# ScalarE rounds the next gate item's weights before it waits for the product

## The reference

```
h = rms_norm(x, ffn_pre_norm[l])
up = dwconv3(h @ w_up[l], ffn_conv_w[l], ffn_conv_b[l])
gate, val = jnp.split(up, 2, axis=-1)
f = (jax.nn.gelu(gate, approximate=True) * val) @ w_down[l]
x = x + rms_norm(f, ffn_post_norm[l])
```

## Time and profile before

| | |
|---|---|
| profiled execution, its time | 1559.35 us |
| its span, first to last instruction | 1557.6 us |
| PE busy | 1450.2 us, 93% |
| DVE busy | 882.8 us, 57% |
| ACT busy | 610.3 us, 39% |
| POOL busy | 520.5 us, 33% |
| mean granted clock of PE | 0.97 of full speed |
| up projection, first layer | about 398 to 652 us |
| up projection, second layer | about 1159 to 1413 us |
| DMA of an item of `w_up`, issue to landing | 3.8 us, median of 88 |

### The profile page before, as it was taken

The page is one execution under the profiler, slowest core; times in us unless marked ns, Lnnn a source line. Parts: engine busy times, 40 slices in busy tenths (PEclk is TensorE's granted clock), DMA queues, the critical chain, the costliest instruction groups (busy, mean ns, idle before and its releaser), DMA issues.

```text
span 1557.6 us, 14970 instructions
## 1 busy us (share of the span) xinstructions
PE 1450.2 (93%) x5815; PEld 1062.1 (68%) x5815; DVE 882.8 (57%) x1001; ACT 610.3 (39%) x859; POOL 520.5 (33%) x243
## 2 busy tenths in 40 slices
PE   5989989988999999999989898999989999999997
PEld 3667756556777777778746675554757777777885
DVE  4765677554676676611175666666456776774112
ACT  5222355643533433422242224556344344333222
POOL 2221311015444344344442122100354344344444
PEclk8999989999999999999989998999999999999998
DMA  7121200002133332323231112000213323322332
GB/s 245 41 57 38 61 28 1 1 28 81 54 87 89 95 90 86 92 88 98 88 126 50 41 45 71 1 0 1 68 41 95 94 83 95 94 82 89 97 95 71
DMA packets 195167, 108.53 MB, mean 70 GB/s; under 512 B 5895, under 2 KB 193657, under 8 KB 194202
## 3 DMA queue, kind: packets, MB, share of 16 engines
q1 hardware_dynamic: 195098, 107.58, 23.4%
HBM read 105.47 MB, written 2.10 MB: 69 GB/s over the span
## 4 chain that ended last, share of the span: by engine, by line
PE 51%; DVE 28%; ACT 14%; issue 5%; POOL 1%; DMA 0%; DVEq 0%; SPq 0%; ACTq 0%; POOLq 0%
PE ps L846 11%; PE ps L848 11%; PE ps L847 11%; DVE cv L1583 11%; ACT cv L753 4%; DVE cv L1586 4%; ACT wh L459 4%; PE ps L1104 3%; PE ps L937 2%; PE ps L824 2%; DVE nm L1485 2%; DVE fprod L1595 2%; PE ps L898 2%; PE ps L924 2%; DVE fl L1597 2%
## 5 line engine op out<-in xcount | busy, mean ns | idle before, releaser
L400 POOL TENSOR_TENSOR wl<-raw,wh 128x1024 fp32r<-128x1024 f32 x184 | 446.1, 2425 | 904.0 <-ACT wh L459 904.0
L846 PE MATMUL ps<-gh,wh 128*128 128x512 f32 x960 | 407.1, 424 | 10.2 <-POOL wl L400 9.2
L847 PE MATMUL ps<-gl,wh 128*128 128x512 f32 x960 | 380.3, 396 | 0.0
L848 PE MATMUL ps<-gh,wl 128*128 128x512 f32 x960 | 380.2, 396 | 0.0
L459 ACT ACTIVATE wh<-raw 128x1024 fp32r<-128x1024 f32 x184 | 193.5, 1052 | 399.5 <-PE ps L848 399.4
L1583 DVE SCALAR_TENSOR_TENSOR cv<-pad,pm,cv 128x512 f32<-128x512 f32 x88 | 179.5, 2040 | 119.2 <-ACT cv L753 119.2
L846 PEld LDWEIGHTS ps<-gh,wh 128*128 128x128 f32 x960 | 180.0, 187 | 83.4 <-issue 39.1
L847 PEld LDWEIGHTS ps<-gl,wh 128*128 128x128 f32 x960 | 180.1, 188 | 53.4 <-issue 12.8
L848 PEld LDWEIGHTS ps<-gh,wl 128*128 128x128 f32 x960 | 179.4, 187 | 45.5
L1215 DVE TENSOR_TENSOR acc<-acc,sq 128x512 f32<-128x512 f32 x24 | 60.5, 2522 | 192.5 <-ACT sq L493 192.3
L846 PE MATMUL ps<-fh,wh 128*128 128x512 f32 x352 | 139.3, 396 | 3.9 <-ACT wh L459 3.0
(11 more groups left out here) (216 smaller groups left out, 1855.1 us busy)
## 6 DMA issues: line engine op xcount, KB each, us to landing
raw<-w_up SPq DMA_DIRECT2D x88, 512.0 KB, 3.8
raw<-w_down SPq DMA_DIRECT2D x32, 512.0 KB, 3.6
raw<-w_in SPq DMA_DIRECT2D x30, 512.0 KB, 3.9
raw<-w_out SPq DMA_DIRECT2D x16, 512.0 KB, 3.7
raw<-w_down SPq DMA_DIRECT2D x16, 384.0 KB, 3.1
xio<-x SPq DMA_DIRECT2D x4, 512.0 KB, 4.3
win<-c_win SPq DMA_DIRECT2D x2, 1024.0 KB, 4.9
TF<-c_tf SPq DMA_DIRECT2D x2, 1024.0 KB, 9.5
```

The source lines that it names most:

```text
L400: nc.gpsimd.tensor_tensor(wl[:, slot, :], raw[:, slot, :], wh[:, slot, :].bitcast(F32), ALU.subtract).then_inc(S["lo_ready"], 1)
L846: mm(ps[0:cols, bank, :], w_hi, x_hi, start=start and k == 0, stop=False)
L847: mm(ps[0:cols, bank, :], w_hi, x_lo, start=False, stop=False)
L848: ins = mm(ps[0:cols, bank, :], w_lo, x_hi, start=False, stop=stop and k == tile_n - 1)
```

## The change

In the first pair ACT's order stays as it was. Behind `tap(1)` of each pair but the last, and ahead of the wait for the product, ACT now makes the high part of the gate item of the pair after next (item `j * 2 + (I_UP + 4)`), which used to be the first instruction of the next pair's round. The same items are rounded in the same order; only the place of `fh` among them is another. `hi` still waits for its raw weights and for PE to be done with the item before in the same slot.

```
-                    hi(lay, j * 2 + (I_UP + 2), 0)
+                    if j == 0:
+                        hi(lay, I_UP + 2, 0)
                     tap(0)
                     act.wait_ge(S["f_conv"], r * 2 + 1)
                     A(gact[:], cv[:, 0, :], ACT.Gelu_apprx_tanh).then_inc(S["f_gelu"], 1)
                     hi(lay, j * 2 + (I_UP + 3), 1)
                     tap(1)
+                    if j < FC - 1:
+                        hi(lay, j * 2 + (I_UP + 4), 0)
                     act.wait_ge(S["f_prod"], r + 1)
                     A(fh[:, j:j + 1, :], fprod[:].rearrange("p (o t) -> p o t", o=1), ACT.Copy).then_inc(S["f_hi"], 1)
```

## The result

The changed kernel takes 1599.5 us (median of 4, 1598.22 to 1601.4) beside 1558.74 us for the kernel before: ratio 1.0263, 95% interval 1.0245 to 1.028. The profiled execution has 1598.47 us and a span of 1596.7 us, 39.1 more than before. So it is slower by 41 us, where 40 were forecast.

The account below looks back on a forecast made before the run. The prediction took a ring over DVE, ACT and POOL (11.66 us a round) as the bound; 21 rounds per layer of 12.04 + 20 x 12.65 add 40.0 us, giving 1599.5 us, range 1590 to 1609.

Parts of the forecast that it names:

- a ring over DVE, ACT and POOL: Up projection: a closed chain of waits not through PE sets the old round at 11.66 us; PE needs 11.20.
- The rounding starts as soon as PE is done with the gate item: ACT's early gate rounding starts 2.98 to 3.10 us into later rounds, 4.17 in the first; formerly 6.22.
- POOL comes 4.10 to 4.22 and ends 7.11 to 7.16: Later rounds: POOL's gate subtraction gets in behind DVE's second tap, so the product ends at 7.66 to 7.71 us.
- Round: One up-projection pass over a value and a gate item: 12.04 us first in each layer, 12.65 later, formerly 11.66.
- product and `fl` held by POOL's subtraction: DVE's two-SBUF-operand instructions wait for all of POOL's subtraction, ending 0.55 us behind it; only `fl` in the first round.
- one case at 107: Old trace: a DVE instruction coming after POOL took 3.42 us instead of 1.22, ending 1.07 behind POOL.
- The first rival: POOL comes ahead of DVE's second tap (L1586), which then waits; round 12.81 us, total 1606; chance 0.22.
- The distance of 0.1: Margin, 0.1 us or less, by which DVE's second tap at 4.10 was to start ahead of POOL.
- The sum: Up-projection rounds of both layers lengthen by 19.8 + 20.2 = 40.0 us, all coming through to the total.
- Means: Sign in the profile: the product's mean time (L1595 before, L1598 after) rises from 0.69 to about 2.7 us.
- PE was to be idle for about 1.3 of each round: Up projection: PE waits 12.65 - 11.3, about 1.3 us a round, at most lowering its clock.
- faster, by PE: POOL doesn't hold product and `fl`, or comes after 6.35; PE bounds at 11.20 us, total 1540; chance 0.06.

Follow-up runs that it names:

- e10_value_first: Kernel before, with the value item's rounding moved ahead of the gelu; 1534.45 us against 1558.93, ratio 0.9843.
- e1_hold: Changed kernel, but POOL also waits for `fl` before subtracting for the next gate item; 1547.72 us, ratio 0.9929 to the kernel before.
- e6_hold_prod: Changed kernel, but POOL waits only for the product before subtracting for the next gate item; 1583.25 us, ratio 1.0160 to the kernel before.
- e2_psum: Changed kernel, but the product takes one factor from PSUM, so its result differs from the reference's; 1548.35 us, ratio 0.9936 to the kernel before.
- e7_layer0: The change in the first layer only, the second keeping the old ACT order; 1579.59 us, ratio 1.0140 to the kernel before.
- e5_all: Changed kernel with POOL waiting for `fl` and the value tap ahead of the value item's rounding; 1553.09 us, ratio 0.9968 to the kernel before.
- e3_swap: Kernel before, with the value tap on ACT put ahead of the value item's rounding; 1545.93 us against 1558.88, ratio 0.9916.
- e4_swap_early: Changed kernel, with the value tap on ACT put ahead of the value item's rounding; 1572.33 us, ratio 1.0087 to the kernel before.

## Why the prediction was right

- **What bounded before**: a ring over DVE, ACT and POOL of 11.66, PE at 11.20. Shown by e10_value_first, where with the ring shorter all rounds but the first of each layer are 11.20.
- **The rounding starts as soon as PE is done with the gate item**: forecast 2.98 to 3.10 in later rounds, 3.03 in the trace. In the first round the forecast was 4.17, behind 408.67; it was 4.16 (407.00 to 411.16).
- **POOL comes 4.10 to 4.22 and ends 7.11 to 7.16; product ends at 7.66 to 7.71**: 4.16, 7.11, 7.66.
- **Round**: forecast 12.65 and 12.04 for the first; 12.65 and 12.07.
- **Cause**: product and `fl` held by POOL's subtraction. This was argued from L1215 and one case at 107, and is shown by e1_hold, e6_hold_prod and e2_psum. The Trainium skill's rule ("SBUF — State Buffer", Who interferes with whom) is that issue order decides who blocks, and that a VectorE instruction with at most one SBUF input, outside the 2-port perf modes, doesn't contend with GpSimd. The first half agrees with e1_hold (POOL behind `fl`: 0.69) and e6_hold_prod (POOL ahead of it: 2.34), the second with e2_psum (0.69 with POOL 0.26 ahead). None of these waits has a semaphore. The opening says that the engines meet only at semaphores; DVE and POOL meet here as well.
- **The first rival**, POOL ahead of the second tap, was real: 4 rounds of 42 at 12.86 or 12.87 (worked out: 12.81). It cost 0.9 us here. The distance of 0.1 was as narrow as the prediction said.
- **The sum**: 40.0 forecast, 40.8 in the rounds, 39.1 between the spans and 40.8 between the medians. That the median is 1599.5 to the tenth is luck: the kernel before came out at 1558.74, 1.0 below the 1559.73 of the opening, and the loss was larger by as much (40.8, where the forecast lies 39.8 above that median).
- **Means**: L1598 2.33 where I wrote about 2.7. That is the length of one held product. Eight of the 44 are free: the first and the last of each layer, and the four behind a held tap. The time was not worked out from this mean.
- **Small slips**, on which the forecast did not hang. In the round of the earlier trace rows the gate evacuation starts 0.08 ahead of the recorded end of `fl` (508.91 and 508.99) and the product 0.11 behind the second tap, so not every row starts 0.02 to 0.1 behind the end of another. PE was to be idle for about 1.3 of each round; by the windows views it was 0.98 (15.42 in 15.67 rounds). The rival "faster, by PE" was also to come if POOL came after 6.35: in e1_hold it comes at 7.13 and the round is 11.44, not 11.20, because of the gate half's first tap.
- **No part came from** the clock (1.00), the transfers or the down projection: the early rounding was released by PE in all 42 rounds and never by a transfer, e7_layer0 lost half, and the stretches behind the rounds kept their length.

## What to carry to other kernels

Moving an instruction into idle time of its own engine also moves what it releases: look at what the released engine will run beside. Where two engines exclude each other, write one round out as a ring with both meetings in it, and count in it who comes first; a start 1.4 us sooner or later decided over 36 us here. A wait for a fast, unrelated engine put ahead of a wait on the ring is free only as long as it is over sooner, and two mends that are each good may spoil that (e5_all).

## What the hardware showed beyond that

- Order at a tie: in the changed kernel and e7_layer0 a second tap that starts 0.06 or 0.07 ahead of POOL by the trace goes first, one that starts 0.04 ahead waits for all 2.39 of it, and 0.05 is found on both sides. So recorded starts this close don't tell which of the two was served first.
- The wait lies inside the recorded duration on both engines: POOL's 2.95 (changed kernel) and 2.80 (e3_swap) against 2.40, DVE's 2.70 against 0.69. A mean that rises in a group with no edit is the sign to look for.
- The held instruction of 128x512 ends 0.53 to 0.56 behind POOL's end in the up projections of every run, whatever it is (tap, product or `fl`). The one of 128x1024 in the earlier trace rows ended 1.07 behind.
- Some of these loops settle into patterns of two rounds: e2_psum 11.3 and 11.6, e4_swap_early 11.9 and 12.2, e5_all 11.4 and 11.6, with the same instructions in each round.
